# Loading the first keys and values of the sample attention during the sparse branch, and what its reordered load queue does

## What is computed

```
ka_all = concat([gather_pages(cache_k_a, page_table), ka_s]);  va_all likewise   # branch A
kb_all = concat([gather_pages(cache_k_b, page_table), kb_s]);  vb_all likewise   # branch B
oa_s = dsa_attend(qa_s, ..., ka_all, va_all, ...)             # softmax over the selected keys
ob_s = stick_breaking_attend(qb_s, ..., kb_all, vb_all, ...)  # log-space cumulative sums
```

## Time and profile before

| | us |
|---|---|
| median of 3 runs (2603.61 to 2608.68) | 2604.2 |
| the profiled execution: time | 2603.99 |
| the profiled execution: span, first to last instruction | 2602.4 |
| `sparse`: first load to last store issued | 1077.7 to 1257.7 |
| `sample_attn`: first instruction to last store issued | 1263.0 to 1479.9 |
| first load of `merge` issued | 1484.7 |

### The profile page before, as it was taken

How to read it: one execution, slowest core, us unless ns; L and a number is a source line. 1 busy time by engine, 2 the same in 40 slices (tenths; PEclk the granted TensorE clock), 3 DMA queues, 4 the chain that set the end, 5 groups by cost and what they waited for, 6 DMA issues and landing times. The chain is left out here.

```text
span 2602.4 us, 37877 instructions
## 1 busy us (share of the span) xinstructions
PE 2258.2 (87%) x13113; PEld 1820.7 (70%) x13113; DVE 1376.3 (53%) x2507; ACT 803.8 (31%) x1349; POOL 139.0 (5%) x226
## 2 busy tenths in 40 slices
PE   3777799999998888788388697968999999999995
PEld 3733588888874445465355486858999999999994
DVE  4316878664654432366244354133666556665666
ACT  4026210211216556566233333122222122212212
POOL 0000000000003443100100000000000000000000
PEclk7988899999998889899799898979999999999998
DMA  3212122222211110211599943102110111111102
GB/s 129 79 32 51 64 102 92 81 97 97 81 52 50 32 35 17 53 36 53 145 354 359 335 124 121 56 22 72 49 48 24 48 48 48 33 40 48 48 16 84
DMA packets 187161, 218.56 MB, mean 84 GB/s; under 512 B 28924, under 2 KB 120956, under 8 KB 185916
## 3 DMA queue, kind: packets, MB, share of 16 engines
q1 hardware_dynamic: 178740, 214.03, 24.9%
q10 hardware_dynamic: 8072, 3.05, 0.5%
q0 software_dynamic: 256, 0.27, 0.1%
HBM read 181.17 MB, written 36.13 MB: 83 GB/s over the span
## 5 line engine op out<-in xcount | busy, mean ns | idle before, releaser
L2242 PE MATMUL ff_up<-m_hi,ff_up_hi 128*128 128x368 f32 x1056 | 348.7, 330 | 14.0 <-DVE ff_up_lo L2330 14.0
L2353 DVE TENSOR_TENSOR x_all<-x_all,ff_down 128x512 f32<-128x512 f32 x396 | 272.4, 688 | 163.5 <-PE ff_down L2257 159.0
L2243 PE MATMUL ff_up<-m_lo,ff_up_hi 128*128 128x368 f32 x1056 | 349.1, 331 | 0.0
L2244 PE MATMUL ff_up<-m_hi,ff_up_lo 128*128 128x368 f32 x1056 | 348.5, 330 | 0.0
L411 PE MATMUL pr_acc<-pr_w_hi,h_hi 128*128 128x512 f32 x720 | 281.0, 390 | 16.2 <-DVE pr_w_lo L352 16.2
L412 PE MATMUL pr_acc<-pr_w_lo,h_hi 128*128 128x512 f32 x720 | 280.8, 390 | 0.0
L413 PE MATMUL pr_acc<-pr_w_hi,h_lo 128*128 128x512 f32 x720 | 280.6, 390 | 0.0
L827 DVE TENSOR_SCALAR_CACHE_REDUCE bi_flags<-scores,bi_thr 128x384 bf16<-128x384 f32 (+6 forms) x252 | 235.4, 992 | 1.3
L2242 PEld LDWEIGHTS ff_up<-m_hi,ff_up_hi 128*128 128x128 f32 x1056 | 199.0, 188 | 15.4 <-DVE ff_up_lo L2330 14.4
L2243 PEld LDWEIGHTS ff_up<-m_lo,ff_up_hi 128*128 128x128 f32 x1056 | 199.1, 189 | 0.9
L2244 PEld LDWEIGHTS ff_up<-m_hi,ff_up_lo 128*128 128x128 f32 x1056 | 199.1, 189 | 0.0
(11 more groups left out here) (288 smaller groups left out, 3799.7 us busy)
## 6 DMA issues: line engine op xcount, KB each, us to landing
out_proj<-pr_staged SPq DMA_DIRECT2D x90, 256.0 KB, 2.0
ff_up_raw<-in_w_up SPq DMA_DIRECT2D x44, 512.0 KB, 4.8
w_raw<-in_w_in SPq DMA_DIRECT2D x10, 2048.0 KB, 7.9
sa_keys<-in_cache_k_a SPq DMA_DIRECT2D x64, 256.0 KB, 4.2
sa_keys<-in_cache_k_b SPq DMA_DIRECT2D x64, 256.0 KB, 7.8
sa_values<-in_cache_v_a SPq DMA_DIRECT2D x64, 256.0 KB, 7.7
sa_values<-in_cache_v_b SPq DMA_DIRECT2D x64, 256.0 KB, 5.4
ff_down_raw<-in_w_down SPq DMA_DIRECT2D x22, 512.0 KB, 3.5
```

Of the source, the lines that this page charges most:

```text
L2242: pe.matmul(up[n][:], w, hi[:, c, at], start=c == 0, stop=False)
L2243: pe.matmul(up[n][:], w, lo[:, c, at], start=False, stop=False)
L2244: ins = pe.matmul(up[n][:], w_rest, hi[:, c, at], start=False, stop=c == KC - 1)
L2353: dve.tensor_tensor(at, at, down[n][:], ALU.add).then_inc(down_added.sem, 1)
```

## The change

A class `SampleLoads` owns the key and value rings, query rows, new rows, masks and page numbers of the sample attention. It is created before `sparse`, with its tiles at the other end of SBUF (`side="right"`). To make room, the scores and the bisection's tiles also go to that end and are released after `stick`. The end of the first `cleanup_on_exit` region moves from after `sparse` to before `stick`.

SP's loop over pairs in `sparse` is unrolled, and after the loads for the next pair it calls `load_ahead(i)`, which issues the page table's numbers, the small loads and the first three halves of keys and values. In `sample_attn` SP starts at half 3, with a new order of keys and values. ACT issues no loads there any more.

```diff
@@ sparse, SP
+            def load_ahead(i):
+                if i == 0:
+                    sp.wait_ge(loads.numbers_in, 16)
+                    numbers.extend(loads.page_numbers(sp, h) for h in range(2))
+                    loads.load_rows(sp, loads.A)
+                    loads.load_rows(sp, loads.B)
+                    loads.load_masks(sp)
+                if i < 3:
+                    loads.load_keys(sp, i, numbers[i % 2])
+                if i >= 1:
+                    loads.load_values(sp, i - 1, numbers[(i - 1) % 2])
             load_rows(0)
-            with sp.Fori(0, PAIRS - 1) as i:
-                body(i, False)
-            body(PAIRS - 1, True)
+            loads.load_numbers(sp)
+            for i in range(PAIRS):
+                body(i, i == PAIRS - 1)
@@ sample_attn, SP
-            load_keys(0)
-            load_keys(1)
-            for h in range(2, HALVES):
-                load_keys(h)
-                load_values(h - 2)
-            load_values(HALVES - 2)
-            load_values(HALVES - 1)
+            for h in range(RING, HALVES):
+                sp.wait_ge(turns[1], page_group(h - RING, PAGES - 1) // 2 + 1)
+                loads.load_keys(sp, h, numbers(h))
+                sp.wait_ge(weighed, h - RING + 1)
+                loads.load_values(sp, h, numbers(h))
@@ sample_attn, ACT
-            for b in range(2):
-                for p in range(PAIRS):
...
-                        act.dma_start(masks[at:at + NQ, :, :], sample_mask.rearrange("(i s q) n -> q i s n", s=2, q=NQ)
-                                      [:, :, s, :]).then_inc(masks_in, 16)
             load_exp_ln(nc, act)
```

More of the change, by code:

```diff
@@ L1256, in _, with sparse @@
                 evacuate(NG - 1)
-def sparse(nc, ctx, proj, ident, masks, out_t):
+def sparse(nc, ctx, proj, ident, masks, out_t, loads):
     def sb(name, shape, dt=F32):
@@ L1322, in body @@
                     load_rows(i + 1)
+                load_ahead(i)
                 sp.wait_ge(o_out.sem, o_out.at(i, NT - 1))
@@ L1479, in sb, with sample_attn @@
+def sample_attn(nc, ctx, loads, own2, spread, mine, strict, forbid, ident, out_ts, next_weights, next_place, next_in):
     def sb(name, shape, dt=F32):
@@ L1485, in sample_attn @@
     A, B = 0, 1
-    COLS = (O_QA, O_KA, O_VA), (O_QB, O_KB, O_VB)
-    NU, RING = NB, 3
-    HALVES = 2 * NU
+    NU, RING, HALVES, IN_HALF = NB, loads.RING, loads.HALVES, loads.IN_HALF
     QUAD = P // PAIRS
-    IN_HALF = 16 * PAGES
-    page_no = sb("page_no", [1, NB * PAGES], I32)
-    q_rows = [sb(f"q_rows{b}", [P, NB // 2, HD]) for b in range(2)]
+    keys, values, q_rows, masks = loads.keys, loads.values, loads.q_rows, loads.masks
+    new_keys, new_values = loads.new_keys, loads.new_values
+    rows_in, masks_in, keys_in, values_in = loads.rows_in, loads.masks_in, loads.keys_in, loads.values_in
     q_t = [[sb(f"q_t{b}_{s}", [P, NB // 2, PAIRS, QUAD]) for s in range(2)] for b in range(2)]
-    masks = sb("masks", [P, NB // 2, SK], BF16)
-    new_keys = [sb(f"new_keys{b}", [NB * NQ, WB]) for b in range(2)]
     new_keys_t = [sb(f"new_keys_t{b}", [P, PAIRS, NB * NQ]) for b in range(2)]
-    new_values = [sb(f"new_values{b}", [P, WB]) for b in range(2)]
-    keys = [sb(f"keys{r}", [P, PAGES, WB]) for r in range(RING)]
-    values = [sb(f"values{r}", [P, PAGES, WB]) for r in range(RING)]
     keys_t = [sb(f"keys_t{c}", [P, PAIRS, 512]) for c in range(2)]
@@ L1549, in _, with numbers @@
         def _(sp):
-            sp.dma_start(page_no[:], pages).then_inc(numbers_in, 16)
-            sp.wait_ge(numbers_in, 16)
             page_regs = {}
-            def load(h, to, cache, sem):
+            def numbers(h):
                 s = 2 * (h // 4) + h % 2
                 if s not in page_regs:
[L1558 to L1572, removed]
-            load_keys(0)
-            load_keys(1)
-            for h in range(2, HALVES):
-                load_keys(h)
-                load_values(h - 2)
-            load_values(HALVES - 2)
-            load_values(HALVES - 1)
+                    page_regs[s] = loads.page_numbers(sp, h)
+                return page_regs[s]
+            for h in range(RING, HALVES):
[3 more added lines that the diff above has]
+                loads.load_values(sp, h, numbers(h))
             for c in range(2 * PAIRS):
@@ L1595, in _ @@
             ins.then_inc(zeroed, 1)
-            pool.wait_ge(rows_in, 16 * (2 * 2 * HEADS + 4))
+            pool.wait_ge(rows_in, loads.ROWS_IN)
             for b in range(2):
@@ L2460, in split_rows @@
             return tuple(ctx.enter_context(nc.sbuf_tensor(f"{name}_{k}", [P, KC, ROWS], F32R)) for k in ("hi", "lo"))
+        load_scope, mask_scope, index_scope = ExitStack(), ExitStack(), ExitStack()
+        scores = index_scope.enter_context(nc.sbuf_tensor("scores", [P, SCORES_W], F32, side="right"))
+        search = Bisection(nc, index_scope, scores)
         with nc.cleanup_on_exit():
[L2464 to L2491, removed]
@@ new lines, in program, with load_first_block @@
+            with ExitStack() as scope:
+                hi, lo = split_rows(scope, "h")
+                w_raw = scope.enter_context(nc.sbuf_tensor("w_raw", [P, KC, 512], F32))
+                raw_in = nc.alloc_semaphore("raw_in")
+                def load_first_block(engine):
+                    col, width, _ = INDEX_PAIR[0]
+                    engine.dma_start(w_raw[:, :, 0:width], a["w_in"].rearrange("(c p) n -> p c n", p=P)
+                                     [:, :, col:col + width]).then_inc(raw_in, 16)
@@ new lines, in program @@
+                with ExitStack() as ctx:
+                    search.semaphores(nc)
+                    projections(nc, ctx, "pr", a["w_in"], a["cos"], a["sin"], hi, lo, w_raw, raw_in, 2, proj,
+                                HEAD_PAIRS, PLAIN_PAIRS, None, search)
+        with nc.cleanup_on_exit():
+            masks = mask_scope.enter_context(nc.sbuf_tensor("masks", [P, MASKS_W], BF16))
+            with index_scope, ExitStack() as ctx:
+                stick(nc, ctx, proj, c["ident"], Selection(nc, ctx, search, masks), sample_mask, out_ts[1])
+            caches = (a["cache_k_a"], a["cache_v_a"]), (a["cache_k_b"], a["cache_v_b"])
+            loads = SampleLoads(nc, load_scope, proj, caches, a["pages"], sample_mask)
+            with ExitStack() as ctx:
+                sparse(nc, ctx, proj, c["ident"], masks, out_ts[0], loads)
+            mask_scope.close()
```

99 lines of the change are left out of this document (73 added, 26 removed).

## The result

| | before | after |
|---|---|---|
| median of 4 runs each | 2604.98 us (2603.61 to 2608.68) | 2695.83 us (2692.99 to 2697.64) |
| profiled execution, span | 2602.4 us | 2691.4 us |

The ratio is 1.0349, with a 95% interval of 1.0336 to 1.0362: slower, 2696 against a forecast of 2692 (2672 to 2714).

What follows compares the result with a forecast made beforehand. It took the steady part of `sample_attn` to have saturated DMA and TensorE busy 111.7 of 131 us. Head -24.7 and iterations +112.6 gave +87.9 on 2604.0: 2692 us, bounds 2678 to 2707, 80% range 2672 to 2714.

Steps and rivals of the forecast that it cites:

- The likeliest case: The forecast's own case for the whole kernel: head gain and longer steady iterations give 2678 to 2707 us, chance 0.82.
- The head: Start of `sample_attn`: waits on small rows and masks go, and keys 3 come in time; -24.7 us.
- The rows' wait: Start of `sample_attn`: POOL no longer idles for the last small rows, so TensorE starts 16.1 us earlier.
- The masks' wait: Start of `sample_attn`: TensorE's 8.59 us wait, through DVE, for the masks goes.
- The iterations: Six steady iterations of `sample_attn`: keys queue behind values that wait for `weighed`; 244.0 us in place of 131.4, +112.6.
- The stops: TensorE idle on keys in `sample_attn`: 12 to 16 us at even halves, 2 to 5 at odd, some 90 in all.
- `sparse`: Added SP loads in `sparse`: `load_ahead(0)` takes 34 us, ending 6 us ahead of the store; cost 0.
- the rival of slow small loads: In `sparse`, strided loads cost SP 1 us each, not 0.4: +14 to +20 us, 2706 to 2712; chance 0.04.
- the 182 that I had named: Sign of a wrong forecast: `sparse` takes over 182 us.
- Cleanup: Clearing moves from one stage border to another: 0, bounded by 1.2 us either way.
- Faster: In `sample_attn`, loads still run ahead, iterations stay at 21.9 us, only the head's gain is left: 2579 us; chance 0.04.
- The low clock for whole iterations: In the steady part of `sample_attn`, TensorE's clock stays low: six times +5.6 us, 2726 us; chance 0.08.

Runs made afterwards that it cites:

- e1: Kernel after, with values again issued two halves behind keys in `sample_attn` and all preloads kept: 2582.60 us, 0.9906 of the kernel before.
- e2: Kernel after, with values issued one half behind keys in `sample_attn`: 2627.84 us, 1.0085 of the kernel before.
- e3: Kernel after, its load order kept, with page numbers of the next two halves read before the wait for `weighed`: 2676.01 us, 1.0267 of the kernel before.
- e6: e1 with the early page-number reads of e3 added: 2584.18 us, 0.9910 of the kernel before.
- e7: e1 without any `load_ahead` in `sparse`, small loads issued from ACT as before: 2612.60 us, 1.0017 of the kernel before.
- e9: e3 with extra identity transposes that keep TensorE busy in its stops: 2677.62 us, 1.0274 of the kernel before.
- e4: Kernel before, with only the order changed to keys h, then values h, nothing preloaded: 2723.65 us, 1.0454 of the kernel before.

## Why the prediction was right

The likeliest case was the one that came, with the mechanism as told. From the profiled execution's 2602.4 to 2691.4 it is 89.0 us against 87.9. That the sum is off by only 1.1 us is partly luck: the iterations cost 3.9 us more than forecast and `sparse` 1.8, while the head and the stage border gave 3.6 more and `sparse` began 1.3 us earlier in this execution. By its terms:

**The head.** Forecast -24.7. From the stage's first instruction to `weigh` in iteration 1 it was 66.8 us (1262.96 to 1329.79) and is 40.7 (1261.21 to 1301.89): -26.1. The rows' wait is right to 0.1 us (25.4 to 9.3). The masks' wait gave 1.4 us more than its own 8.6. What that stop also took was the clock behind it, here in busy time by stretch right after the restart, before:

```profile
1299.00:1303.00 4.00, 3.17 (x14) 2.81 (x15) 1.50 (x3) 0.60 (x1) 0.00 (x0) 0.50 0.89 337
```

The granted clock was 0.50 there, the 1.2 GHz level; in after's 1276 to 1280 it is 1.00. I had counted such a loss behind every new stop and not behind the one that goes. That the clock makes these 1.4 us is read from the traces; no run tests it. Keys 3, issued at 1281.63, came in time: no stop on them.

**The iterations.** Forecast +112.6, measured +116.5 (247.9 for 244.0). Its three parts, mean of six: keys `2u+3` landing after the values' issue 31.6 us with new numbers (31.0 forecast) and 26.0 without (25.3); from there to `weigh` 10.57 (10.53); from `weigh` to the values' issue 1.99 (1.99). The 3.9 us are nearly all in the landing, six times about 0.6. Keys `2u+2`, which the forecast had at 17.7 and 14.1, landed 18.2 to 19.8 and 14.2 to 16.2 us after the values' issue; this is absorbed, since the odd keys come last.

**The stops** add up to 110 us, where I named some 90: those at even halves are 12.3 to 17.9 us (12 to 16 forecast), those at odd ones 2.5 to 4.1 (2 to 5). The sum didn't use that figure.

**`sparse`.** Forecast 0. Its loads ran as worked out (SP's timeline, after):

```profile
1087.95 0.60 SPq L1315 DMA_DIRECT2D sp_k_rows<-out_proj  x1
...
1111.62 5.96 SPq L1541 DMA_DIRECT2D sa_masks<-sample_mask  x16
1117.79 4.96 SPq L1551 DMA_DIRECT2D sa_keys<-in_cache_k_a  x8
1129.37 0.33 SPq L1325 DMA_DIRECT2D out_t_a<-sp_o_all  x1
```

34 us, through at 1122.75, 6.6 ahead of the store; the rival of slow small loads is out (0.37 us each). From the first value rows' issue to the last store `sparse` takes 180.4 us (178.6 before), 1.8 that I had at 0. The value rows were issued 1.3 us earlier in this execution, which `stick` before it gave (its last store of a tile is issued 1.9 us earlier), so it ends 0.5 later. From its first load, as in the table ahead of the rows, it is 182.5 us (1075.63 to 1258.14) against 180.0: that is over the 182 that I had named as a sign of being wrong, and with the same `sparse` four of the experiments lie over it by either measure (e1, e2, e3, e6). So the 0 was too low in five of the six traces with this `sparse`, by 1.8 to 5.1 us. That the loads make it is not shown: e7, with none of them in `sparse`, takes 180.7 us there, and e9, with all of them, 178.6.

**Cleanup.** Forecast 0, within 1.2 either way. The gap from the last store to the next stage is 3.1 us (1258.14 to 1261.21), 5.3 before: 2.2 less. At the border that the clearing moved to, ahead of `stick`, the first load is issued 0.5 us later (779.16, before 778.68), and nothing is left of that inside `stick`: its first store after 930 us is issued at 930.55, before at 930.56.

The sum: +0.5 - 2.2 - 26.1 + 116.5 = +88.7 at the first load of `merge` (1573.45, before 1484.7), +89.0 at the end.

**The rivals.** "Faster" hung on intervals under 26 us: 37.9 to 45.1 came, and with another queue order the same kernel is the faster one at 2583, near its 2579. The low clock for whole iterations would have shown `weigh` far more than 10.5 us behind the odd restart; it was 9.3 to 11.7. The Trainium skill ("Trainium Kernel Development and Optimization", "Best Practices") advises to double-buffer so that DMA overlaps compute. The runs bear that out only where the issue runs ahead: with the same three buffers for each, TensorE stood 5.7 us for keys in e1, 104 in e4 and 110 in after.

## What to carry to other kernels

A ring of buffers is refilled only as far ahead as the issuing queue gets: where one in-order queue fills two rings that are freed at different points, put the load whose buffer comes free latest last, behind all that is already free (2583 us against 2696 here with the same buffers). Moving loads into an idle stage pays above all for what the start of the next waits for: here small rows and masks brought 18 of 29 us, and 12.6 MB of keys and values, with their page numbers, the other 10. Read registers and page numbers before the wait, not between the issues behind it: that is worth 20 us where the queue is late, and nothing where it runs ahead.

## What the runs showed of the hardware

DMA engines can be full at a third of the rate that they reach with large pages. In e1, while the small strided pieces of masks and rows were worked off, the busy time by stretch was:

```profile
1125.00:1130.00 5.00, 4.64 (x90) 4.16 (x86) 0.59 (x2) 1.24 (x6) 0.00 (x0) 1.00 1.08 120
```

A share of 1.08 moved 120 GB/s, where much the same share (1.05) moved 401 in large pages; in e6 it was 1.10 and 121 GB/s over the same 5 us. Keys issued behind them in e1 landed in 7.6 to 12.4 us, and the value rows in 9.2, though SP had issued all of it on time. How full it gets differs between executions of the same loads: in after these keys landed in 6.0 to 6.9 us and the value rows in 5.5.

Stops of TensorE of nearly one length left different clocks behind them. Busy time by stretch, kernel after, behind stops of 4.12, 2.62 and 2.47 us:

```profile
1335.00:1340.00 5.00, 4.65 (x20) 3.20 (x24) 1.38 (x2) 2.14 (x3) 0.07 (x1) 0.50 0.00 0
1374.00:1379.00 5.00, 4.72 (x32) 2.85 (x32) 1.38 (x2) 1.19 (x2) 0.00 (x0) 0.66 0.00 0
1459.00:1464.00 5.00, 4.50 (x44) 3.13 (x42) 2.00 (x3) 1.79 (x3) 0.00 (x0) 1.00 0.01 3
```

The first fell to the 1.2 GHz level, the last kept 2.4 GHz, and the second, 0.15 us longer than the last, fell for a part of the stretch. Ahead of an odd half, each such fall costs 1.2 to 2.4 us to the next `weigh` (9.3 without, 10.5 to 11.7 with). The length of the stop alone doesn't decide it: in the kernel before a stop of 2.48 us was followed by 0.50, and in e9 one of 1.96 us by a fall to 0.50 and 10.8 us to `weigh`. What does, the runs don't show.
